# Feed-forwards on Trainium2: all up tiles before all down tiles, and each high weight streaming both parts as 512 columns

## The chip, the cores and the metric

One core of one Trainium2 chip runs the kernel. The metric is the device time of one execution in microseconds, as the median of runs. TensorE multiplies matrices (a weight load and a matmul are two instructions; results go to the banks of PSUM, `ps` in the kernel, eight banks of 128 x 512 fp32), VectorE and ScalarE work element by element, SyncE issues the DMAs of the weights.

## The reference

Two chains of layers over 256 tokens of width 1024, all in fp32: a block with a gated feed-forward, a hybrid attention mixer, cross attention and a second gated feed-forward, and then an RWKV layer, a squared-ReLU feed-forward, a sliding-window attention and a second squared-ReLU feed-forward. What matters here are the four feed-forwards:

```
x = x + 0.5 * swiglu(rmsnorm(x, ffn1_norm), w_gate, w_up, w_down)    # D_FF = 2816, again as ffn2
swiglu(h, w_gate, w_up, w_down) = (silu(h @ w_gate) * (h @ w_up)) @ w_down
x = x + square(relu(rms_norm(x, ln_mlp) @ w1)) @ w2                  # FFN_DIM = 4096, mlp1 and mlp2
```

## The kernel before

Activations are kept turned: 128 channels on the partitions, tokens along a row, `e.x` as 8 chunks of 128 x 256. Every weight comes as a tile of 1 MB (128 x 2048 fp32) in one fixed stream of 204 tiles. `feed` (L253) issues the DMAs from SyncE into a ring of four tiles; each waits until the tile four places earlier has been split (L263). To keep fp32 accuracy with the faster format `fp32r`, every number is split in two parts: ScalarE copies half a tile (1024 columns) into `tile_hi` (`heads_after`, L295, instruction L305) and VectorE subtracts that from the tile to give `tile_lo` (`rests_after`, L310, instruction L315). There are `SPLIT = 4` slots of half a tile, so a split waits until TensorE is done with the half tile four halves earlier. Activations (`hT`, the normed input, and `hidden`, the inner values) are split in the same way.

`product` (L353 to L357) is the core: three matmuls for one chunk of 128 weights rows and 128 weight columns, high by high, high weights by low activations, low weights by high activations, each with a weight load of its own and 256 columns, all three summed in the same half of a bank. The names in the profile give the activation first and the weight second (`ps<-hT_lo,tile_hi`). A tile has 16 products, 48 matmuls.

`ffn_stage` (L651) does a feed-forward in steps of 256 inner channels: 11 in ffn1 and ffn2 (a gate tile, an up tile, a down tile for each), 16 in mlp1 and mlp2 (an up tile and a down tile). The down tile of step j follows the up tiles of step j + 2 (`LAG = 2`), so up and down tiles take turns; the stream of weights has the same order. The up results of a step lie in one bank for each tile (banks 0 to 3), the down results add up in banks 4 to 7 over the whole stage. The inner values of three steps are kept (`hid`, `depth = 3`).

Gated: VectorE multiplies the gate's bank by the token's norm factor (L768), ScalarE takes Silu (L726), VectorE scales the up bank (L771) and multiplies the two (L774). Squared ReLU: ScalarE takes Relu out of the bank (L731), VectorE scales (L780) and squares (L781). Then ScalarE makes the high part (L736) and VectorE the low one (L789). All engines work in the order in which the program is written, so a split between two of these steps stands in the line with them.

At the end, the last down tile goes through the banks in pairs of output chunks, four blocks. For each block VectorE adds the bank to `e.x` (`add_to_residual`, L514 or L516), ScalarE makes the next section's high input and the squares (L548, L554), VectorE the low input (`rest_of_gained`, L524). The next section's first product waits for the first block's low input (`x_arrives`), its second tile's middle for the sum of squares (L597, L599, asked for by TensorE at L608).

Of the kernel before, what the change touches and what calls it, by code (L numbers as in the profile page):

```python
# [49 lines left out]
LAG = 2  # L50
# [8 lines left out]
AT_WEIGHTS, AT_MOVING, AT_INPUT, AT_FIRST_SLOT = 224, 160, 160, 128  # L59
# [84 lines left out]

class Unit:
# [18 lines left out]
def build(nc, a, out):  # L164
    ctx = ExitStack()
    with ctx:
# [19 lines left out]
        def over(name, tensor, shape, dtype=F32):  # L186
            return nc.alloc_sbuf_tensor_at(f"{name}{nc.next_id()}", shape, dtype, offset=places[tensor.name])

        def pair(stack, name, shape, place=AT_MOVING):
            return tuple(sb(stack, f"{name}_{part}{nc.next_id()}", shape, F32R, place) for part in ("hi", "lo"))  # L190
# [9 lines left out]
        e.hT = pair(ctx, "hT", [P, KC, SEQ], AT_INPUT)  # L200
        e.spare = tuple(over("spare", part, [P, KC, SEQ]) for part in e.hT)
# [4 lines left out]
        e.w_hi, e.w_lo = pair(ctx, "tile", [P, SPLIT, HALF], AT_WEIGHTS)  # L206
# [25 lines left out]
        ffn_stage(e, "mlp2", D_FF2, False, 1.0, None)  # L232
# [62 lines left out]
def heads_after(e, act, done):  # L295

    while may_split(e.hi_issued, done):
# [7 lines left out]
        act.activation(e.w_hi[:, n % SPLIT, :], e.ring[:, tile % RING, span(n % 2, HALF)],  # L305
# [4 lines left out]
def rests_after(e, dve, done):  # L310

    while may_split(e.lo_issued, done):
        n = e.lo_issued
        dve.wait_ge(e.tile_hi.handle, n + 1)
        dve.tensor_tensor(e.w_lo[:, n % SPLIT, :], e.ring[:, CUT[n // 2] % RING, span(n % 2, HALF)],  # L315
                          e.w_hi[:, n % SPLIT, :].bitcast(F32), ALU.subtract).then_inc(e.tile_lo.handle, 1)
        e.lo_issued += 1
# [12 lines left out]
def arrived(e, pe, g, half):  # L330

    n = 2 * place_in_cut(g) + half
    pe.wait_ge(e.tile_lo.handle, n + 1)
    return e.w_hi[:, n % SPLIT, :], e.w_lo[:, n % SPLIT, :]


def chunks_of(pair):
    return tuple(part.rearrange("p (k n) -> p k n", k=KC) for part in pair)
# [14 lines left out]
def product(pe, out, left, right, start, stop):  # L353

    pe.matmul(out, left[0], right[0], start=start, stop=False)  # L355
    pe.matmul(out, left[0], right[1], start=False, stop=False)  # L356
    return pe.matmul(out, left[1], right[0], start=False, stop=stop)  # L357
# [10 lines left out]
def cut(pair, *index):  # L368
    return tuple(part[index] for part in pair)
# [31 lines left out]
def col_to_natural(e, pe, g, src, bank):  # L401
# [3 lines left out]
    w = tuple(part[:, n:n + 2, :].rearrange("p m (k n) -> p m k n", k=KC) for part in (e.w_hi, e.w_lo))  # L405
# [100 lines left out]
def add_to_residual(e, dve, b, scale, last_tile, bank=4):  # L506
# [3 lines left out]
    else:  # L510
        multiplied(e, dve, last_tile)
    xs = e.x[:, two(b), :].rearrange("p m n -> p (m n)")
# [16 lines left out]
def tail_vector(e, dve, scale, outs, last_tile, bank=4):  # L529


    for n in range(6 if outs else 4):
        if n < 4:
            add_to_residual(e, dve, n, scale, last_tile, bank)
# [116 lines left out]
def ffn_stage(e, section, width, gated, scale, outs):  # L651
# [5 lines left out]
    per = 3 if gated else 2  # L657
    g0 = FIRST[section]
    depth = 3
    act_done, whole_ready, hi_ready, hidden_ready, scaled, chain = (  # L660
        e.sig(x) for x in ("gate_ready", "hidden_whole_ready", "hidden_hi_ready", "hidden_ready", "gate_scaled", "dve_step"))
    hT = e.hT

    def up_tile(j, which):
        return g0 + (per - 1) * j + max(j - LAG, 0) + which

    def down_tile(j):
        return g0 + (per - 1) * min(j + LAG + 1, steps) + j

    def up_bank(j, which):  # L670

        return 2 * (j % 2) + which if gated else (0, 2, 1, 3)[j % 4]

    end = down_tile(steps - 1)
    all_squared = e.sig("squared").since(4)

    with Open(nc) as block, ExitStack() as stack:
        hid = [e.pair(stack, f"hidden{n}", [P, 2, SEQ], AT_MOVING if n else AT_FIRST_SLOT) for n in range(depth)]
        whole = e.sb(stack, f"hidden_whole{nc.next_id()}", [P, 2, 2 * SEQ])
        tmp = e.sb(stack, f"gate{nc.next_id()}", [P, 2, 2 * SEQ])  # L680

        def slot(part, j):
            return hid[j % depth][part][:, :, :].rearrange("p m n -> p (m n)")

        @block.sync
        def _(sp):
            feed(e, sp, g0 + per * steps)

        @block.tensor
        def _(pe):  # L690
            def down(j):
                pe.wait_ge(*hidden_ready.at(j + 1))
                row_to_T(e, pe, down_tile(j), hid[j % depth], 0, j == 0, j == steps - 1)

            for j in range(steps):
                if gated and j >= 2:

                    pe.wait_ge(*hidden_ready.at(j - 1))
                if not gated and j >= 4:

                    pe.wait_ge(*act_done.at(j - 3))
                for which in range(per - 1):
                    nth = (per - 1) * j + which
                    if nth == 0:
                        first_to_T(e, pe, up_tile(j, which), hT, up_bank(j, which))
                    elif nth == 1:
                        col_to_T(e, pe, up_tile(j, which), hT, up_bank(j, which), between=lambda: scale_sums(e, pe, 7))
                        scale_spread(e, pe, 7)
                    else:
                        col_to_T(e, pe, up_tile(j, which), hT, up_bank(j, which))  # L710
# [2914 lines left out]
```

## Time and profile before

| | us |
|---|---|
| median of 3 runs | 1413.38 (1409.81 to 1413.94) |
| span of the profiled execution | 1422.4 |
| what lies around the span of that execution | not given by the page |
| TensorE busy | 1372.8 (97%), 12692 matmuls |
| TensorE's weight loads busy | 1314.1 (92%) |
| VectorE busy | 913.7 (64%) |
| ScalarE busy | 706.0 (50%) |
| read from HBM | 219.55 MB, 155 GB/s over the span |

The profile is of one execution, whose span is 9.0 us longer than the median of the runs. Busy time is the union of an engine's instructions; matmuls overlap in it, so how often one starts (count over the length of a window) says more than how long one lasts. A row of the timeline gives start, length, engine, line, operation, output and inputs, count of merged instructions, and in brackets the idle time before it and what ended that. In the stretches used here the granted TensorE clock is 1.00 of 2.4 GHz.

### The profile page before, as it was taken

The page shows a single profiled execution, that of the slowest core. Times are in us where ns is not written, and L with a number is a line of the kernel's source. Part 1 is how long each engine was busy: PE and PEld are TensorE (multiplying, and loading weights), DVE is VectorE, ACT ScalarE, POOL GpSimd, SP SyncE. Part 2 cuts the span into 40 slices and gives each one's busy share as a digit, 9 for nine tenths or more (in the row PEclk, how much of TensorE's full clock was granted, in tenths as well). Part 3 has the DMA queues.
Part 4 walks back from the last instruction along what each step waited for, and adds up shares of the span by engine and source line. Part 5 has one row for each costly group of instructions (what it writes and reads, how often), then busy time and mean ns, then how long its engine had stood idle before and what let it go on. Part 6 is the DMA issues. An engine that isn't in the chain of part 4 may idle for free. (4 is left out here: it accounts for less than half of the span.)

```text
span 1422.4 us, 28871 instructions
## 1 busy us (share of the span) xinstructions
PE 1372.8 (97%) x12692; PEld 1314.1 (92%) x12692; DVE 913.7 (64%) x1419; ACT 706.0 (50%) x1098; POOL 8.2 (1%) x14
## 2 busy tenths in 40 slices
PE   7999999999899999999999899999999996999999
PEld 7999999888799999999998677889999995999999
DVE  4665566557785546666588763667666668666664
ACT  5444455356564446444458333446444466554442
POOL 0000000000000000000000010000000000000000
PEclk9999999999999999999999998999999999999999
DMA  7555555461344344655524021114555541255552
GB/s 272 208 179 191 194 180 179 182 264 60 119 178 178 129 151 156 214 182 197 199 85 176 31 91 60 61 60 167 190 197 207 190 149 60 94 204 178 178 184 84
DMA packets 33109, 222.48 MB, mean 156 GB/s; under 512 B 3879, under 2 KB 5295, under 8 KB 6616
## 3 DMA queue, kind: packets, MB, share of 16 engines
q1 hardware_dynamic: 31928, 219.57, 42.7%
q8 instruction: 100, 1.64, 0.4%
q10 hardware_dynamic: 1056, 1.07, 0.2%
q14 instruction: 25, 0.20, 0.0%
HBM read 219.55 MB, written 1.07 MB: 155 GB/s over the span
## 5 line engine op out<-in xcount | busy, mean ns | idle before, releaser
L315 DVE TENSOR_TENSOR tile_lo<-ring,tile_hi 128x1024 fp32r<-128x1024 f32 x388 | 466.0, 1222 | 276.8 <-ACT tile_hi L305 276.2
L305 ACT ACTIVATE tile_hi<-ring 128x1024 fp32r<-128x1024 f32 x388 | 399.5, 1053 | 250.8 <-PE ps L357 245.8
L355 PE MATMUL ps<-hT_hi,tile_hi 128*128 128x256 f32 x1664 | 467.5, 281 | 5.0 <-DVE tile_lo L315 1.8
L356 PE MATMUL ps<-hT_lo,tile_hi 128*128 128x256 f32 x1664 | 463.4, 278 | 0.0
L357 PE MATMUL ps<-hT_hi,tile_lo 128*128 128x256 f32 x1664 | 463.4, 278 | 0.0
L355 PEld LDWEIGHTS ps<-hT_hi,tile_hi 128*128 128x128 f32 x1664 | 315.0, 189 | 10.6 <-issue 4.6
L356 PEld LDWEIGHTS ps<-hT_lo,tile_hi 128*128 128x128 f32 x1664 | 312.9, 188 | 0.0
L357 PEld LDWEIGHTS ps<-hT_hi,tile_lo 128*128 128x128 f32 x1664 | 312.7, 188 | 0.0
L355 PE MATMUL ps<-hidden_hi,tile_hi 128*128 128x256 f32 x864 | 241.2, 279 | 0.0
L357 PE MATMUL ps<-hidden_hi,tile_lo 128*128 128x256 f32 x864 | 241.2, 279 | 0.0
L356 PE MATMUL ps<-hidden_lo,tile_hi 128*128 128x256 f32 x864 | 241.2, 279 | 0.0
L355 PEld LDWEIGHTS ps<-hidden_hi,tile_hi 128*128 128x128 f32 x864 | 163.5, 189 | 0.0
L356 PEld LDWEIGHTS ps<-hidden_lo,tile_hi 128*128 128x128 f32 x864 | 162.4, 188 | 0.0
L357 PEld LDWEIGHTS ps<-hidden_hi,tile_lo 128*128 128x128 f32 x864 | 162.3, 188 | 0.0
L736 ACT ACTIVATE hidden_hi<-hidden_whole 128x512 fp32r<-128x512 f32 x54 | 34.2, 633 | 114.1 <-DVE hidden_whole L774 65.8
L789 DVE TENSOR_TENSOR hidden_lo<-hidden_whole,hidden_hi 128x512 fp32r<-128x512 f32 x54 | 37.4, 692 | 39.3 <-ACT hidden_hi L736 26.2
L780 DVE TENSOR_TENSOR hidden_whole<-gate,token_scale 128x512 f32<-128x512 f32 x32 | 22.1, 692 | 32.4 <-ACT gate L731 32.4
L731 ACT ACTIVATE gate<-ps 128x512 f32<-128x512 f32 x32 | 19.0, 595 | 42.8 <-PE ps L357 42.8
L1064 ACT ACTIVATE scores<-scores,lane_stats 128x128 f32<-128x128 f32 (+3 forms) x80 | 35.4, 445 | 8.8 <-DVE lane_stats L1090 8.8
L355 PE MATMUL ps<-y_turned,tile_hi 128*128 128x256 f32 x128 | 35.8, 280 | 2.9 <-DVE tile_lo L315 2.9
L726 ACT ACTIVATE gate<-gate 128x512 f32<-128x512 f32 x22 | 13.9, 632 | 46.1 <-DVE gate L768 46.1
L356 PE MATMUL ps<-y_turned,tile_hi 128*128 128x256 f32 x128 | 35.4, 277 | 0.0
(467 smaller groups left out, 1997.5 us busy)
## 6 DMA issues: line engine op xcount, KB each, us to landing
ring<-stream SPq DMA_DIRECT2D x204, 1024.0 KB, 4.8
x_sb<-x SPq DMA_DIRECT2D x4, 256.0 KB, 4.0
bias<-f_dram ACTq DMA_DIRECT2D x1, 1024.0 KB, 8.1
fox_bias<-forget_dram SPq DMA_DIRECT2D x1, 1024.0 KB, 6.2
squares<-mem SPq DMA_DIRECT2D x1, 1024.0 KB, 4.7
out<-x_sb SPq DMA_DIRECT2D x4, 256.0 KB, 2.2
const_sb<-const SPq DMA_DIRECT2D x1, 581.0 KB, 9.8
small_sb<-small SPq DMA_DIRECT2D x1, 493.5 KB, 9.5
```

Source lines behind the costliest of these rows:

```text
L305: act.activation(e.w_hi[:, n % SPLIT, :], e.ring[:, tile % RING, span(n % 2, HALF)], ACT.Copy).then_inc(e.tile_hi.handle, 1)
L315: dve.tensor_tensor(e.w_lo[:, n % SPLIT, :], e.ring[:, CUT[n // 2] % RING, span(n % 2, HALF)], e.w_hi[:, n % SPLIT, :].bitcast(F32), ALU.s ...
L355: pe.matmul(out, left[0], right[0], start=start, stop=False)
L356: pe.matmul(out, left[0], right[1], start=False, stop=False)
L357: return pe.matmul(out, left[1], right[0], start=False, stop=stop)
L726: act.activation(tmp[:, j % 2, :], tmp[:, j % 2, :], ACT.Silu).then_inc(*act_done.one())
L731: act.activation(tmp[:, j % 2, :], e.ps[:, up_bank(j, 0), :], ACT.Relu).then_inc(*act_done.one())
L736: act.activation(slot(0, j), whole[:, j % 2, :], ACT.Copy).then_inc(*hi_ready.one())
L780: link.done(dve.tensor_tensor(halves_of(both), halves_of(tmp[:, j % 2, :]), scale_pairs(e), ALU.mult))
L789: dve.tensor_tensor(slot(1, j), both, slot(0, j).bitcast(F32), ALU.subtract).then_inc(*hidden_ready.one())
L1064: x = act.activation(summed(step)[:, lane], summed(step)[:, lane], ACT.Exp, bias=st[:, 0, lane:lane + 1], accum_out=st[:, 1, lane:lane + 1])
```

## The change

The four feed-forwards run all up tiles first and then all down tiles, and the weight stream is laid out so. The inner values of every step are kept (`hidden`, 11 or 16 steps, high and low part side by side). High and low parts of all activations now lie one behind the other in one tensor (`Pair`), so one matmul can read both. `wide_product` loads the high weights once and streams 512 columns, the high and the low activations, into the two halves of a bank; a second matmul loads the low weights and streams the 256 high columns into the first half. A result thus takes a whole bank, and its two halves have to be added: for an up tile ScalarE copies the second half out and VectorE adds the first, before the scaling; at the end of the stage `add_to_residual` adds both halves to `x`, one after the other. Up tiles go round through all eight banks in four pairs, and the down results take all eight. Squared ReLU is now a maximum and scaling on VectorE and a Square on ScalarE. All other sections keep `product`; in the sliding-window stage three banks are renumbered.

```diff
+def wide_product(pe, bank, left, right, start, stop):
+    def low(stop):
+        return pe.matmul(bank[:, 0:SEQ], left.lo, right.hi, start=False, stop=stop)
+    if stop:
+        low(False)
+    mm = pe.matmul(halves_of(bank), left.hi, right.both, start=start, stop=stop)
+    return mm if stop else low(False)
...
+    if wide:                                   # add_to_residual
+        xs = e.x[:, two(b), :]
+        for half in range(2):
+            x = dve.scalar_tensor_tensor(out=xs, in0=e.ps[:, pair_of(b), span(half, SEQ)], scalar=scale, in1=xs,
+                                         op0=ALU.mult, op1=ALU.add)
+            if half == 0:
+                Chain(dve, e.sig("dve_step")).done(x)
+        x.then_inc(*e.sig("residual_added").one())
+        return
...
+def pair_of(n, first=0):
+    at = 2 * ((n + first) % 4)
+    return slice(at, at + 2)
...
         def _(pe):                             # ffn_stage, TensorE
+            first_up()
+            up(1, between=lambda: scale_sums(e, pe, scale_bank))
+            scale_spread(e, pe, scale_bank)
+            for n in range(2, count):
+                if n == 3:
+                    pe.wait_ge(*e.sig("scale_ready").at(1))
+                if n >= 4:
+                    pe.wait_ge(*summed.at(n - 3))
+                up(n)
...
+            halves = [arrived(e, pe, down0, k) for k in range(2)]
+            pe.wait_ge(*hidden_ready.at(1))
+            up_last = [max(n for n in range(count) if bank_of(m) in range(8)[up_banks(n)]) for m in range(KC)]
+            for m in sorted(range(KC), key=lambda m: up_last[m]):
+                pe.wait_ge(*summed.at(up_last[m] + 1))
+                for k in range(2):
+                    mm = down(halves[k], k, 0, m, start=k == 0)
+            mm.then_inc(*e.tile_done.one(2))
+            for j in range(1, steps - 1):
                 pe.wait_ge(*hidden_ready.at(j + 1))
...
+            def copy_low(n):                   # ScalarE
+                tile_after(e, act, g0 + n)
+                if n >= 2:
+                    act.wait_ge(*(consumed if gated else whole_ready).at(n - 1))
+                act.activation(part[:, n % 2, :, :], e.ps[:, up_banks(n), SEQ:2 * SEQ], ACT.Copy).then_inc(*low_copied.one())
+                heads_after(e, act, 2 * (g0 + n) + 2)
...
+                    copy_low(2 * j)
+                    act.wait_ge(*consumed.at(2 * j + 1))
+                    act.activation(gate[:, j % 2], gate[:, j % 2], ACT.Silu).then_inc(*act_done.one())
+                copy_low(ups * j + ups - 1)
                 act.wait_ge(*whole_ready.at(j + 1))
+                if not gated:
+                    act.activation(whole[:, j % 2], whole[:, j % 2], ACT.Square).then_inc(*act_done.one())
+                    act.wait_ge(*act_done.at(j + 1))
+                act.activation(hidden[:, j, 0], whole[:, j % 2], ACT.Copy).then_inc(*hi_ready.one())
...
+            def add_low(n):                    # VectorE
+                rests_before(e, dve, g0 + n + 1)
+                dve.wait_ge(*low_copied.at(n + 1))
+                dve.tensor_tensor(part[:, n % 2], e.ps[:, up_banks(n), 0:SEQ], part[:, n % 2], ALU.add).then_inc(*summed.one())
+                dve.wait_ge(*summed.at(n + 1))
...
+                    add_low(2 * j)
+                    dve.tensor_tensor(gate[:, j % 2], part[:, 0], scale_pairs(e), ALU.mult).then_inc(*consumed.one())
+                    rests_after(e, dve, 2 * (g0 + 2 * j) + 2)
+                    add_low(2 * j + 1)
+                    dve.tensor_tensor(whole[:, j % 2], part[:, 1], scale_pairs(e), ALU.mult).then_inc(*consumed.one())
...
+                    add_low(j)
+                    dve.scalar_tensor_tensor(out=whole[:, j % 2], in0=part[:, j % 2], scalar=0.0, in1=scale_pairs(e),
+                                             op0=ALU.max, op1=ALU.mult).then_inc(*whole_ready.one())
+                rests_after(e, dve, 2 * (g0 + ups * (j + 1)))
                 dve.wait_ge(*hi_ready.at(j + 1))
+                dve.tensor_tensor(hidden[:, j, 1], whole[:, j % 2], hidden[:, j, 0].bitcast(F32),
                                   ALU.subtract).then_inc(*hidden_ready.one())
```

## Rows read from the trace of the kernel before

**Rows 1.** The page, part 1: busy us of each engine, share of the span, instructions.
```profile
PE 1372.8 (97%) x12692; PEld 1314.1 (92%) x12692; DVE 913.7 (64%) x1419; ACT 706.0 (50%) x1098; POOL 8.2 (1%) x14
```

**Rows 2.** Windows inside ffn1, ffn2, mlp1, mlp2: length, busy us (instructions) by engine.
```profile
core 0: us, PE busy (x) PEld busy (x) DVE busy (x) ACT busy (x) POOL busy (x), PEclk, DMA share, GB/s
60.00:180.00 120.00, 120.00 (x1020) 120.00 (x1019) 71.41 (x71) 51.03 (x56) 0.00 (x0) 1.00 0.53 189
560.00:700.00 140.00, 140.00 (x1232) 140.00 (x1232) 88.32 (x90) 63.59 (x71) 0.00 (x0) 1.00 0.56 196
1000.00:1120.00 120.00, 120.00 (x1054) 120.00 (x1054) 75.30 (x78) 57.79 (x66) 0.00 (x0) 1.00 0.53 193
1270.00:1400.00 130.00, 130.00 (x1105) 130.00 (x1105) 79.46 (x81) 60.35 (x70) 0.00 (x0) 1.00 0.50 179
```

**Rows 3.** Timeline, TensorE or its loads, three places, plain fp32: start, length, count.
```profile
258.92 3.59 PE L1281 MATMUL ps<-bias,flip_sb 128*128 128x512 f32 x8
...
800.10 4.94 PEld L2258 LDWEIGHTS ps<-ring,mixed_values 128*128 128x128 f32 x23
...
498.21 1.03 PE L1791 MATMUL ps<-const_sb,bias 128*128 128x128 f32 x8
```

**Rows 4.** Groups by line and shape, plain fp32 matmuls: busy us, mean ns.
```profile
L1281 PE MATMUL ps<-bias,flip_sb 128*128 128x512 f32 x8 | 3.6, 592 | 0.0
...
L1791 PE MATMUL ps<-const_sb,bias 128*128 128x128 f32 x16 | 2.1, 272 | 0.0
```

**Rows 5.** Timeline of TensorE and its loads in an up tile of ffn1.
```profile
60.03 0.28 PE L355 MATMUL ps<-hT_hi,tile_hi 128*128 128x256 f32 x1
60.04 0.19 PEld L356 LDWEIGHTS ps<-hT_lo,tile_hi 128*128 128x128 f32 x1
```

**Rows 6.** Timeline of TensorE's loads, mixer stage, loads of 32 columns.
```profile
227.71 0.11 PEld L356 LDWEIGHTS ps<-hT_lo,misc_hi 128*32 128x32 f32 x1
227.82 0.11 PEld L357 LDWEIGHTS ps<-hT_hi,misc_lo 128*32 128x32 f32 x1
```

**Rows 7.** Groups by line and shape: count | busy us, mean ns | idle before them.
```profile
L315 DVE TENSOR_TENSOR tile_lo<-ring,tile_hi 128x1024 fp32r<-128x1024 f32 x388 | 466.0, 1222 | 276.8 <-ACT tile_hi L305 276.2
L789 DVE TENSOR_TENSOR hidden_lo<-hidden_whole,hidden_hi 128x512 fp32r<-128x512 f32 x54 | 37.4, 692 | 39.3 <-ACT hidden_hi L736 26.2 <-PE ps L357 13.1
...
L514 DVE TENSOR_TENSOR x_sb<-ps,x_sb 128x512 f32<-128x512 f32 x24 | 16.1, 687 | 10.2 <-PE ps L357 10.2
...
L305 ACT ACTIVATE tile_hi<-ring 128x1024 fp32r<-128x1024 f32 x388 | 399.5, 1053 | 250.8 <-PE ps L357 245.8 <-DMA ring<-stream 3.3 <-PEq L2432 1.5
L736 ACT ACTIVATE hidden_hi<-hidden_whole 128x512 fp32r<-128x512 f32 x54 | 34.2, 633 | 114.1 <-DVE hidden_whole L774 65.8 <-DVE hidden_whole L781 48.2
...
L731 ACT ACTIVATE gate<-ps 128x512 f32<-128x512 f32 x32 | 19.0, 595 | 42.8 <-PE ps L357 42.8
L554 ACT ACTIVATE squares<-x_sb 128x512 f32<-128x512 f32 x32 | 19.0, 617 | 1.7 <-DVE x_sb L516 1.7
```

**Rows 8.** Timeline around the end of ffn1: VectorE, then TensorE.
```profile
199.68 1.28 DVE L516 SCALAR_TENSOR_TENSOR x_sb<-ps,x_sb 128x512 f32<-128x512 f32 x2
201.69 0.69 DVE L516 SCALAR_TENSOR_TENSOR x_sb<-ps,x_sb 128x512 f32<-128x512 f32 x1 [0.72 <-PE ps L357]
...
203.71 2.46 DVE L524 SCALAR_TENSOR_TENSOR hT_lo<-x_sb,small_sb,hT_hi 128x256 fp32r<-128x256 f32 x6
...
203.31 0.36 PE L355 MATMUL ps<-hT_hi,tile_hi 128*128 128x256 f32 x1 [0.25 <-DVE hT_lo L524]
```

**Rows 9.** Timeline of the sum of squares after ffn1: VectorE, then TensorE.
```profile
209.77 0.69 DVE L599 TENSOR_TENSOR squares<-squares 128x512 f32<-128x512 f32 x1
...
211.57 0.95 PE L608 MATMUL ps<-ones,squares 128*128 128x1 f32 x8
```

**Rows 10.** Timeline at the end of mlp2: VectorE, then TensorE.
```profile
1419.43 0.69 DVE L514 TENSOR_TENSOR x_sb<-ps,x_sb 128x512 f32<-128x512 f32 x1 [0.73 <-PE ps L357]
...
1419.12 0.28 PE L357 MATMUL ps<-hidden_hi,tile_lo 128*128 128x256 f32 x1
```

More of the change, by code:

```diff
@@ L49 @@
 LEAST = -3e38
-LAG = 2
 RING = 4
@@ L368, in cut @@
 def cut(pair, *index):
-    return tuple(part[index] for part in pair)
+    both = None if pair.both is None else pair.both[(index[0], slice(None), *index[1:])]
+    return Pair(pair.hi[index], pair.lo[index], both)
 ALL = slice(None)
@@ L648, in halves_of, with bank_of, ffn_stage @@
     return bank.rearrange("p (m n) -> p m n", m=2)
-def ffn_stage(e, section, width, gated, scale, outs):
+def pair_of(n, first=0):
+    at = 2 * ((n + first) % 4)
+    return slice(at, at + 2)
+def bank_of(m, first=0):
+    return pair_of(m // 2, first).start + m % 2
+def ffn_stage(e, section, width, gated, scale, outs, first=0):
     e.stage()
@@ L656, in ffn_stage @@
     steps = width // 256
[L657 removed]
+    ups = 2 if gated else 1
     g0 = FIRST[section]
[L659 to L668 removed]
@@ L685, in _ @@
         @block.sync
         def _(sp):
-            feed(e, sp, g0 + per * steps)
+            feed(e, sp, end + 1)
         @block.tensor
         def _(pe):
-            def down(j):
-                pe.wait_ge(*hidden_ready.at(j + 1))
[L693 to L710, printed above, removed]
-                if j >= LAG:
-                    down(j - LAG)
@@ L713, in _, with up @@
-            mark_tail(e)
-            for j in range(steps - LAG, steps):
-                down(j)
+            def up(n, between=None):
+                for m in range(2):
+                    w = chunks_of(arrived(e, pe, g0 + n, m))
+                    for k in range(KC):
+                        mm = wide_product(pe, e.ps[:, bank_of(2 * (n % 4) + m, first), :], cut(w, ALL, k, ALL),
+                                          cut(hT, ALL, k, ALL), k == 0, k == KC - 1)
+                    mm.then_inc(*e.tile_done.one())
+                    if between and m == 0:
+                        between()
@@ L717, in _ @@
+            mark_tail(e)
+            pe.wait_ge(*hidden_ready.at(steps))
+            halves = [arrived(e, pe, end, k) for k in range(2)]
+            for m in range(KC):
+                for k in range(2):
+                    mm = down(halves[k], k, steps - 1, m, stop=k == 1)
+                if m % 2 == 1 and m < KC - 1:
+                    mm.then_inc(*e.sig("acc_ready").one())
+            mm.then_inc(*e.tile_done.one(2))
         @block.scalar
```

167 lines of the change are left out of this document (78 added, 89 removed).

## The prediction

> **What bounds the kernel now.** I read the page's busy shares first: TensorE 97%, its weight loads 92%, VectorE 64%, ScalarE 50% [rows 1]. TensorE bounds the kernel, and the question is what one of its instructions costs. So I cut out four stretches that lie wholly inside the four feed-forwards and counted matmuls [rows 2]. The reader is to see two prices there for the same instruction. In ffn1 and mlp2 a matmul of 256 columns starts every 120/1020 us = 117.6 ns and 130/1105 us = 117.6 ns; in ffn2 and mlp1 every 140/1232 us = 113.6 ns and 120/1054 us = 113.9 ns. The granted clock is 1.00 (2.4 GHz) in all four, and TensorE never idles in them, so I have no reason for the difference and carry both. 256 columns at 2.4 GHz are 106.7 ns. A matmul therefore costs 10.9 or 7 ns more than its columns, and a product (three matmuls) 352.9, 340.9, 341.6 and 352.9 ns in ffn1, ffn2, mlp1 and mlp2.
>
> **What the change does to a product.** It keeps the 768 columns and turns three pairs of load and matmul into two: high weights with 512 columns, low weights with 256. There are 33 tiles in each gated feed-forward and 32 in each other, 16 products each: 528, 528, 512, 512, together 2080 products. Each loses one load and one matmul start. What that is worth hangs on what the 7 to 11 ns are. The trace has no matmul of 512 columns with this number format, so I bound it.
>
> The nearest rows are plain fp32 matmuls, which take two clocks a column. Eight of 512 columns take 3.59 us [rows 3]; less the length of the last one, 0.59 [rows 4], that is 3.00/7 = 429 ns from start to start. 23 loads under 256-column matmuls take 4.94 us, (4.94 − 0.19)/22 = 216 ns apart; 8 matmuls of 128 columns (1.03 − 0.27)/7 = 109 ns [rows 3, 4]. Their columns alone are 426.7, 213.3 and 106.7 ns, so 2.3 to 2.7 ns are added whatever the length. The middle one is the important one: its stream is exactly as long as that of a 512-column matmul of this kernel (213.3 ns), a 128x128 load runs under it, and it costs 216 ns. A load lasts 0.19 us from its start a few ns after the matmul before began [rows 5], so under 213 ns of stream it is over in time and under 107 ns it is not. That makes the 7 to 11 ns a load that comes a little late. After the change the load of the low weights hides under the 512 columns; only the load of the next high weights stays under 256. Then a product is 216 + 113.6 = 329.6 ns in the quick stretches and 216 + 117.6 = 333.6 ns in the slow ones.
>
> Against this speaks that matmuls with only 32 weight columns, whose loads last 0.11 us, also start 0.11 us apart [rows 6]: the added time doesn't shrink with the load. If it is a fixed price of each matmul of this format, a product saves just one of it, 6.9 to 10.9 ns. I keep this as a rival. The bounds of the price are: nothing saved (the excess goes with columns), and 216 + 109 = 325 ns (both matmuls lose it). I take 329.6 and 333.6, since the one row whose stream has the right length says 216.
>
> Saved on products: ffn1 528 × (352.9 − 333.6) = 10.2 us; ffn2 528 × (340.9 − 329.6) = 6.0; mlp1 512 × (341.6 − 329.6) = 6.1; mlp2 512 × 19.3 = 9.9. Sum 32.2 us.
>
> The Trainium skill (TensorE: Matmul & The Clock Gate, "Back-to-back issue gap") has a rule that speaks against such a gain: a warm matmul costs its columns over 2.4 GHz plus about 2.5 ns. By it three times 256 columns are 327.5 ns and 512 with 256 are 325, only 2.5 ns saved a product, 5 us in all. The trace agrees with the rule in plain fp32 [rows 3] and not in the feed-forwards, at 340.9 to 352.9 ns; by the rule, what stands above it there is something that the change need not touch.
>
> **VectorE and ScalarE while up tiles run.** Before, a third or half of the tiles are down tiles, which ask only for splits. Now all up tiles come in a row, and the low sums add work. VectorE's operations on 512 elements cost 0.69 us, whether from the banks or not; a split half 1.22; ScalarE's split half 1.05, its copy from the banks 0.60, its others 0.62 to 0.63 [rows 7].
> Squared ReLU, one up tile: VectorE 2 × 1.22 + 3 × 0.69 (sum, max-and-scale, low half) = 4.5 us; ScalarE 2 × 1.05 + 0.60 + 0.62 + 0.63 = 4.0 us; TensorE 16 × 0.330 = 5.3 us. Gated, two up tiles: VectorE 4 × 1.22 + 6 × 0.69 = 9.0, ScalarE 6.7, TensorE 10.6. Both fit, at 85% of VectorE. The closed round is longer than the work, as both engines wait for each other in order. For squared ReLU it is: sum 0.69, scale 0.69, ScalarE's square 0.63 and high half 0.63, next split's high half 1.05, VectorE's low half 1.22: 4.9 us (handovers between the engines not counted), 0.4 less than TensorE's 5.3. For a gated step the round adds up to 3 × 0.69 (second sum, scaling, product), 0.63, 1.05, 1.22, 2 × 0.69 (first sum, scaling), 0.63, 1.05, 1.22: 9.3 against 10.6. TensorE doesn't wait for a tile's sum until four tiles later (eight banks in four pairs), and a split is due 1.5 tiles after its slot is free. So I cost this at nothing, with TensorE's stream as its cover; if the round were longer than a tile, each of the 76 up tiles (22 + 22 + 16 + 16) would cost the excess.
>
> **From up to down.** The first down tile takes the pairs of banks in the order in which they are freed; the last pair is asked for after three others, 12 products = 4.0 us after the last up tile, and its copy and sum take 0.60 + 0.69 and up to one split half in between, 1.05: under 2.6 us. The last inner value is due ten or more tiles later. Nothing. The down tiles leave VectorE 2.4 us in 5.3. The stream of weights is 1 MB a tile; 5.3 us a tile asks 198 GB/s, and such stretches ran at 179 to 196 with the DMA engines busy 50 to 56% of the time [rows 2]. The queue waits for the split of four tiles before, as it did, now with nothing else between. Nothing.
>
> **The end of each feed-forward.** Here the change costs. A pair of banks now needs two additions to x, the second waiting for the first: one more of 0.69 us in each of four blocks. At ffn1's end VectorE goes from its first addition at 199.68 to the last low half at 206.17 with 0.72 us idle; the next section's first product comes at 203.31 after a wait for the first low half [rows 8]. That one stands behind three additions, now six: 3 × 0.69 − 0.72 = 1.4 us later. Everything after on VectorE is 4 × 0.69 − 0.72 = 2.1 us later, and the sum of squares, which TensorE asks for at 211.57 [rows 9], is ready at 210.46 before and 212.6 after, when TensorE asks at 213.0: no second stall. mlp1's end has the same form. So 1.5 us each, 3.0. ffn2 has no such overlap: its sums of squares stand behind the last addition, 1.0 us (0.69, and some backlog, as two additions, 1.38, no longer fit in 4 × 0.333 = 1.33 us of TensorE). At mlp2's end the output leaves after the last addition, which before began at 1419.43 behind the last matmul at 1419.12 [rows 10]: 0.9 us. Sum 4.9 us.
>
> **Sum.** 1422.4 − 32.2 + 4.9 = 1395.1 us, 27.3 less. The profiled span is 9.0 us longer than the median of the runs, 1413.4, and the page gives no other time for it; I take the difference over: 1386 us.
>
> **Rivals.**
> 1. Each matmul has a fixed price beyond its columns. The 32-column loads speak for it, the 216 ns against. Saved: 528 × 10.9 + 528 × 6.9 + 512 × 7.2 + 512 × 10.9 = 18.7 us, less 4.9: 1400 us.
> 2. The excess goes with the columns (say, how fast they are read), or is something that the change doesn't touch. Nothing is saved, 4.9 lost: 1418 us. For it: the excess is the same for 32 and 128 weight columns. Against: plain fp32 adds 2.3 to 2.7 ns at every length [rows 3], not a share of it. The mild form: a product saves only that price of one matmul, 2.5 ns × 2080 = 5.2 us, and the time stays at 1413 us. This is also where the rule of the Trainium skill cited above (TensorE: Matmul & The Clock Gate) would end.
> 3. VectorE and ScalarE bound the up tiles: slower, where the mechanism is the closed round, its place the 76 up tiles. It decides from an excess of 27.3/76 = 0.36 us a tile, a round of 5.7 us for squared ReLU; for an excess of 0.6 us a tile it costs 46 and ends at 1432. Against: idle time stands before most splits now (276 us of VectorE behind ScalarE's high half), for: that idle time is partly this round.
> 4. All stretches become quick ones and both matmuls lose their excess, 325 ns a product: 528 × 27.9 + 528 × 15.9 + 512 × 16.6 + 512 × 27.9 = 45.9 us, less 4.9: 1372 us.
>
> **How the numbers follow.** The forecast has 0.50, the fixed price 0.20, rival 4 0.08, the columns 0.10 (half of it the mild form), the engines 0.12. A difference of 0.3% (4.2 us) is about what a measurement can tell from no change. Faster: forecast, fixed price and rival 4, 0.78, and 0.02 of the engines, with an excess well under 0.36 us: 0.80. Same: the mild form 0.05 and 0.02 of the engines: 0.07. Slower: the columns' 0.05 and the engines' 0.08: 0.13. The range goes from 1374, near rival 4, to 1411, short of the columns' case, and leaves out about 0.2.
>
> **What would show it.** 512-column matmuls 216 ns apart from the next, the 256-column ones 113 to 118; at 224 and 114 to 118 the fixed price is right, at 227 to 235 the columns. TensorE without idle time in the stretches of up tiles, VectorE there at 80 to 88%; a wait of TensorE for the low half of a split in them shows rival 3. The next section's first product 1.4 us later behind the last matmul of ffn1 and mlp1. Wrong would be the forecast also if the slow price of ffn1 and mlp2 moved to the others, 4 ns in each of two matmuls of 1040 products: up to 8 us.

## The result and the profile after

The changed kernel takes 1441.64 us (median of 4 runs, 1438.63 to 1447.47), the kernel before beside it 1413.66 (4 runs, 1409.81 to 1416.64): ratio 1.020, 95% interval 1.0167 to 1.0233. It is 28 us slower; the forecast was 27 us faster. The profiled execution of the changed kernel took 1447.47 us, 1.3 more than its span of 1446.2; by span it is 23.8 us longer than the one before.

The page, part 1 [rows 1]:

```profile
PE 1390.4 (96%) x10612; PEld 1235.9 (85%) x10612; DVE 950.2 (66%) x1479; ACT 751.3 (52%) x1174; POOL 8.2 (1%) x14
```

2080 matmuls and as many loads are gone (12692 to 10612), and TensorE is busy for longer. Windows inside the feed-forwards, two for each (up tiles, then down tiles) in the order ffn1, ffn2, mlp1, mlp2, with the columns of [rows 2]:

```profile
60.00:130.00 70.00, 70.00 (x399) 60.95 (x398) 53.42 (x61) 38.86 (x50) 0.00 (x0) 1.00 0.56 187
150.00:190.00 40.00, 40.00 (x229) 34.77 (x228) 17.36 (x15) 15.28 (x15) 0.00 (x0) 1.00 0.56 188
560.00:650.00 90.00, 90.00 (x513) 78.39 (x512) 72.64 (x85) 52.59 (x68) 0.00 (x0) 1.00 0.58 199
680.00:720.00 40.00, 40.00 (x229) 34.73 (x228) 17.58 (x15) 14.85 (x14) 0.00 (x0) 1.00 0.56 188
1000.00:1060.00 60.00, 60.00 (x342) 52.27 (x341) 49.46 (x57) 41.30 (x57) 0.00 (x0) 1.00 0.59 201
1080.00:1150.00 70.00, 70.00 (x398) 60.77 (x398) 30.62 (x25) 25.92 (x26) 0.00 (x0) 1.00 0.56 191
1290.00:1340.00 50.00, 50.00 (x286) 43.50 (x285) 41.37 (x48) 35.03 (x47) 0.00 (x0) 1.00 0.58 192
1370.00:1430.00 60.00, 60.00 (x341) 52.14 (x340) 26.31 (x22) 22.28 (x21) 0.00 (x0) 1.00 0.42 141
```

A product is now two matmuls, so by these counts it costs between 2 × 40/229 = 349 ns and 2 × 60/341 = 352 ns. A window also counts the matmuls that reach in over its edge, which makes short windows read 1 to 4 ns low; from the first start to the last one the trace gives 352.4 to 352.5 ns a product in the up tiles and 353.3 in the down tiles of all four. Before it was 352.9, 340.9, 341.6 and 352.9 ns [rows 2], by counts as well. TensorE has no idle time in any of them, and VectorE is busy 76 to 83% in the up tiles. The timeline of TensorE in an up tile of ffn1 shows which of the two matmuls is dear:

```profile
60.01 0.28 PE L382 MATMUL ps<-hT_pair,tile_pair 128*128 128x256 f32 x1
60.13 0.40 PE L386 MATMUL ps<-hT_pair,tile_pair 128*128 128x512 f32 x1
60.36 0.28 PE L382 MATMUL ps<-hT_pair,tile_pair 128*128 128x256 f32 x1
60.48 0.40 PE L386 MATMUL ps<-hT_pair,tile_pair 128*128 128x512 f32 x1
```

From a 512-column start to the next matmul 0.23 to 0.24 us, from a 256-column one 0.12. The prediction's text names this case: 512 columns at 227 to 235 ns mean that "the columns" is right.

The end of ffn1, VectorE and then TensorE, answers to [rows 8, 9]:

```profile
199.81 4.05 DVE L547 SCALAR_TENSOR_TENSOR x_sb<-ps,x_sb 128x512 f32<-128x512 f32 x6
203.78 0.87 DVE L565 SCALAR_TENSOR_TENSOR hT_pair<-x_sb,small_sb,hT_pair 128x256 fp32r<-128x256 f32 x2
204.57 1.41 DVE L547 SCALAR_TENSOR_TENSOR x_sb<-ps,x_sb 128x512 f32<-128x512 f32 x2
...
202.72 0.39 PE L386 MATMUL ps<-hidden,tile_pair 128*128 128x512 f32 x1
204.81 0.35 PE L372 MATMUL ps<-hT_pair,tile_pair 128*128 128x256 f32 x1 [1.70 <-DVE hT_pair L565]
...
206.83 0.39 PE L372 MATMUL ps<-hT_pair,tile_pair 128*128 128x256 f32 x1 [0.37 <-DVE hT_pair L565]
```

Six additions in a row stand ahead of the first low half, as predicted, and TensorE's wait grows from 0.25 to 1.70 us. A second wait comes at 206.83, behind the last two additions. At the end of mlp1 the first wait is the same, and there the clock falls after it (timeline of TensorE, then a window of the changed kernel and one of the kernel before at the same place in the program):

```profile
1154.88 0.39 PE L386 MATMUL ps<-hidden,tile_pair 128*128 128x512 f32 x1
1156.97 0.36 PE L372 MATMUL ps<-kvT_pair,tile_pair 128*128 128x256 f32 x1 [1.70 <-DVE kvT_pair L565]
...
1157.00:1171.00 14.00, 14.00 (x73) 14.00 (x74) 10.88 (x20) 8.06 (x16) 0.00 (x0) 0.56 0.38 142
```

```profile
1141.00:1149.00 8.00, 8.00 (x70) 8.00 (x71) 7.94 (x17) 8.00 (x16) 0.00 (x0) 1.00 0.40 133
```

73 matmuls took 14 us at a granted clock of 0.56, mostly the lower level of 1.2 GHz; before, 70 took 8 us at 1.00. The difference is 14 − 73 × 8/70 = 5.7 us.

Where the 23.8 us of span came from, read off the same landmarks (starts of the same instructions) in both timelines: 2.4 by the sum of squares after ffn1 (asked for at 214.00, before at 211.57), 1.8 more by the start of ffn2 (a half-clock spell near 428 us is longer), 4.6 in ffn2, 5.6 in mlp1, 1.6 at its end, 6.1 in the section of shared keys and values behind it, 1.7 in mlp2 and the end of the kernel. The last ffn1 matmul begins at the same time as before, 202.72 against 202.78: where the old price was already the slow one, the wide product changed next to nothing.

### The profile page after: what moved, and what is told of

Same layout as the page of the kernel before. It is cut to its first block and busy times, and to the rows that moved or that the text cites. A ratio compares the mean times of both kernels' runs of the same rounds, so it can differ in the third digit from the quotient of the medians.

```text
span 1446.2 us, 24871 instructions
## 1 busy us (share of the span) xinstructions
PE 1390.4 (96%) x10612; PEld 1235.9 (85%) x10612; DVE 950.2 (66%) x1479; ACT 751.3 (52%) x1174; POOL 8.2 (1%) x14
## 5 line engine op out<-in xcount | busy, mean ns | idle before, releaser
L331 DVE TENSOR_TENSOR tile_pair<-ring,tile_pair 128x1024 fp32r<-128x1024 f32 x388 | 470.4, 1222 | 294.3 <-ACT tile_pair L321 293.6
L321 ACT ACTIVATE tile_pair<-ring 128x1024 fp32r<-128x1024 f32 x388 | 405.2, 1055 | 282.2 <-PE ps L382 164.1
L386 PE MATMUL ps<-hT_pair,tile_pair 128*128 128x512 f32 x1216 | 421.6, 397 | 1.7 <-DVE tile_pair L331 0.8
L382 PE MATMUL ps<-hT_pair,tile_pair 128*128 128x256 f32 x1216 | 317.6, 281 | 0.0
L386 PE MATMUL ps<-hidden,tile_pair 128*128 128x512 f32 x864 | 303.3, 397 | 0.0
L386 PEld LDWEIGHTS ps<-hT_pair,tile_pair 128*128 128x128 f32 x1216 | 219.3, 188 | 45.4 <-issue 2.7
L382 PEld LDWEIGHTS ps<-hT_pair,tile_pair 128*128 128x128 f32 x1216 | 228.3, 188 | 12.7
L382 PE MATMUL ps<-hidden,tile_pair 128*128 128x256 f32 x864 | 237.5, 281 | 0.0
L386 PEld LDWEIGHTS ps<-hidden,tile_pair 128*128 128x128 f32 x864 | 160.4, 188 | 37.2
L382 PEld LDWEIGHTS ps<-hidden,tile_pair 128*128 128x128 f32 x864 | 162.2, 188 | 2.8
L372 PE MATMUL ps<-hT_pair,tile_pair 128*128 128x256 f32 x448 | 128.3, 286 | 4.7 <-DVE hT_pair L565 2.1
L373 PE MATMUL ps<-hT_pair,tile_pair 128*128 128x256 f32 x448 | 125.3, 280 | 0.0
L374 PE MATMUL ps<-hT_pair,tile_pair 128*128 128x256 f32 x448 | 125.3, 280 | 0.0
L372 PEld LDWEIGHTS ps<-hT_pair,tile_pair 128*128 128x128 f32 x448 | 84.9, 189 | 9.6 <-issue 4.9
L843 DVE TENSOR_TENSOR up_part<-ps,up_part 128x512 f32<-128x512 f32 x76 | 52.5, 690 | 52.7 <-ACT up_part L805 52.6
L373 PEld LDWEIGHTS ps<-hT_pair,tile_pair 128*128 128x128 f32 x448 | 84.9, 189 | 0.0
L374 PEld LDWEIGHTS ps<-hT_pair,tile_pair 128*128 128x128 f32 x448 | 84.8, 189 | 0.0
L805 ACT ACTIVATE up_part<-ps 128x512 f32<-128x512 f32 x76 | 45.2, 595 | 70.5 <-PE ps L386 70.5
```

Source lines behind the costliest of these rows:

```text
L321: act.activation(e.w.hi[:, n % SPLIT, :], e.ring[:, tile % RING, span(n % 2, HALF)], ACT.Copy).then_inc(e.tile_hi.handle, 1)
L331: dve.tensor_tensor(e.w.lo[:, n % SPLIT, :], e.ring[:, CUT[n // 2] % RING, span(n % 2, HALF)], e.w.hi[:, n % SPLIT, :].bitcast(F32), ALU.s ...
L372: pe.matmul(out, left.hi, right.hi, start=start, stop=False)
L373: pe.matmul(out, left.hi, right.lo, start=False, stop=False)
L374: return pe.matmul(out, left.lo, right.hi, start=False, stop=stop)
L382: return pe.matmul(bank[:, 0:SEQ], left.lo, right.hi, start=False, stop=stop)
```

## The experiments

Two theories stood at the start. The forecast's: an added time of 7 to 11 ns for each load that is not hidden. Its rival: a price that goes with the columns. To them came a question that the trace raised: why ffn2 and mlp1 lost what they had.

**1. The price by itself.** A kernel that leaves the computation out and only runs short streams of matmuls of this number format, most of them 8 products long, with operands at many positions in SBUF (0 to 224 bytes past a multiple of 256) and nothing else going on. Its kinds, in short:

```diff
+if kind == "three":   # high*high, high*low, low*high, 256 columns each
+elif kind == "wide":  # high * (high and low), 512 columns; low * high, 256
+elif kind == "only512":
+elif kind == "cols":  # 256 columns, but 32 or 64 weight columns
```

> Leaves the whole computation out; it only streams fp32r matmuls with nothing else running: three matmuls of 256 columns per product, 512 with 256, 512 alone, 256 columns with 32 to 128 weight columns, 32 to 256 columns with 128 weight columns, at several positions of the operands in their rows. Theory C (the price goes with the columns): 512 alone starts every 226 to 236 ns, exactly twice 256 alone (113 to 118), with 128 or 32 weight columns alike. Theory of the forecast (a late load): 512 every 216 ns, 256 with 32 weight columns 109. A fixed price: 512 every 220 to 224. If the position of the operands chooses between the quick price (113.3) and the slow one (117.8), each price keeps to its positions; if it is a state that lasts, the same positions show both.

Measured from start to start: three of 256 columns 113.3 to 120.2 ns each, by position and by what ran before (the same operands gave 118 ns at first and 113.3 in eleven repeats after a pause); the wide product 346 to 356 ns, so at none of 24 pairs of positions at the 340 of the quick stages, but at eight of them at 346 to 347; 512 columns alone 229 to 235 at seven positions and 227 at the eighth. Here is the wide product at one of the eight pairs:

```profile
280.43 0.28 PE L52 MATMUL ps<-mvg,wtf 128*128 128x256 f32 x1
280.54 0.39 PE L51 MATMUL ps<-mvg,wtf 128*128 128x512 f32 x1
280.77 0.28 PE L52 MATMUL ps<-mvg,wtf 128*128 128x256 f32 x1
280.89 0.39 PE L51 MATMUL ps<-mvg,wtf 128*128 128x512 f32 x1
```

With 256 columns and only 32 weight columns it is 113.8 ns at one position and 120.0 at another, where 128 weight columns gave 114.0 and 116.8. So a load of a quarter of the size saves nothing and a 512-column stream costs about what two of 256 do. The late load is out, and both prices exist without any other engine at work.

**2. The wide product alone undone**, halves and sums kept:

```diff
-    mm = pe.matmul(halves_of(bank), left.hi, right.both, start=start, stop=stop)
+    pe.matmul(bank[:, 0:SEQ], left.hi, right.hi, start=start, stop=False)
+    mm = pe.matmul(bank[:, SEQ:2 * SEQ], left.hi, right.lo, start=False, stop=stop)
```

> The changed kernel with the wide product alone undone: three matmuls of 256 columns again, the low activations by the high weights still into the second half of the bank, all else as changed. Theory C: the same time as the changed kernel within 5 us, so 1436 to 1447, since the columns are the same; less by up to 12 us if ffn2 and mlp1 fall back to the quick price. Theory of the forecast: 2080 loads more that come late, 11 to 19 ns each, so 1465 to 1480.

1428.3 us (6 runs, 1416.77 to 1433.51), ratio 1.0056 (1.0006 to 1.0107): 13 us less than the changed kernel by medians, 20 by ratios, which is the fairer measure, since the two ran beside different runs of the kernel before. Windows of ffn1 and ffn2, then the one behind mlp1's end:

```profile
60.00:130.00 70.00, 70.00 (x597) 70.00 (x596) 53.52 (x62) 39.24 (x49) 0.00 (x0) 1.00 0.52 183
560.00:650.00 90.00, 90.00 (x797) 90.00 (x796) 74.03 (x85) 54.01 (x70) 0.00 (x0) 1.00 0.58 205
...
1142.00:1156.00 14.00, 14.00 (x73) 14.00 (x72) 10.41 (x19) 7.96 (x16) 0.00 (x0) 0.54 0.38 140
```

ffn1 runs at 117.3 ns, ffn2 at 112.9 (the two others as ffn2). More loads, more matmuls, and faster; the forecast's theory had asked for 1465 to 1480. VectorE and ScalarE have the same work as in the changed kernel, so they are not what slowed it. The last row: mlp1's end kept its wait (1.82 us idle here) and the low clock behind it.

**3. Up tiles wide, down tiles as three matmuls in one half**, with one addition at the end:

```diff
-                return wide_product(pe, e.ps[:, bank_of(m), :], ...)          # down
+                return product(pe, e.ps[:, bank_of(m), 0:SEQ], ...)
-        for half in range(2):
-            x = dve.scalar_tensor_tensor(out=xs, in0=e.ps[:, pair_of(b), span(half, SEQ)], ...)
+        x = dve.scalar_tensor_tensor(out=xs, in0=e.ps[:, pair_of(b), 0:SEQ], ...)
```

> The changed kernel with down tiles as three matmuls of 256 columns into one half of each bank, so that a block needs one addition to x again; up tiles stay wide. Theory C: down tiles cost the same, the ends of the feed-forwards get back 1.5 to 2.5 us each, and the idle time of 2 us before the shared keys and values, after which TensorE runs at half clock, shrinks to 0.5: 6 to 14 us less than the changed kernel, 1427 to 1435. If the half clock stays, 1435 to 1438. Theory of the forecast: 864 products lose 11 to 19 ns each, 9 to 16 us more, less the same 6 to 14: about the same time as the changed kernel.

1424.95 us (10 runs, 1422.36 to 1431.57), ratio 1.0049 (1.0022 to 1.0075), 2 us below the 1427 to 1435 of theory C. Windows of ffn1 and mlp1, up and down:

```profile
60.00:130.00 70.00, 70.00 (x399) 60.92 (x399) 53.41 (x63) 39.76 (x50) 0.00 (x0) 1.00 0.56 193
150.00:190.00 40.00, 40.00 (x355) 40.00 (x355) 17.64 (x16) 15.94 (x15) 0.00 (x0) 1.00 0.60 207
...
1000.00:1060.00 60.00, 60.00 (x342) 52.27 (x341) 49.45 (x57) 41.52 (x56) 0.00 (x0) 1.00 0.57 198
1080.00:1130.00 50.00, 50.00 (x443) 50.00 (x442) 22.57 (x19) 19.62 (x19) 0.00 (x0) 1.00 0.56 193
```

In one execution and one feed-forward, the wide half costs 2 × 70/399 = 351 ns a product and the other 3 × 40/355 = 338 (352.5 and 340.0 from start to start). This is the clearest pair of rows of the study: the price changes where the form of the product does. It also refutes one line of theory C, that down tiles cost the same either way: all four down halves ran at 340.0.

**4. The order alone**: all up tiles, then all down tiles, every product three matmuls into one half, no copies, no sums, one addition.

```diff
-                        mm = wide_product(pe, e.ps[:, bank_of(...), :], ...)
+                        mm = product(pe, e.ps[:, bank_of(...), 0:SEQ], ...)
-                act.activation(part[:, n % 2, :, :], e.ps[:, up_banks(n), SEQ:2 * SEQ], ACT.Copy)...
-                dve.tensor_tensor(part[:, n % 2], e.ps[:, up_banks(n), 0:SEQ], part[:, n % 2], ALU.add)...
```

> The order alone: all up tiles, then all down tiles, inner values kept, but every product three matmuls into one half of a bank, no copy and no sum of halves on ScalarE and VectorE, one addition to x. Theory C: as the kernel before within 5 us where the price of a column is as before; up to 13 us more if ffn2 and mlp1 keep the slow price, 1410 to 1427. If waits of VectorE and ScalarE in the up tiles were the cause of the loss, this is 20 us or more faster than the run with only the down tiles changed.

1413.0 us (10 runs, 1407.34 to 1421.75), ratio 0.9959 (0.9932 to 0.9986), up and down tiles of all four feed-forwards at 113.3 ns a matmul from start to start. The order costs nothing, so all of the loss is in the wide product and its halves.

**5. Long streams.** 144 matmuls after each short pause, four pairs of positions, computation left out again:

> Leaves the whole computation out; long runs of products after a pause, nothing else running, at four pairs of operand positions that were quick or slow for 256 columns: three matmuls of 256 into one half; the wide product of the changed kernel; the wide product with the low weights first; 512 alone; three matmuls of 256 into two halves. Theory P (the quick price of 0.443 ns a column is a rhythm between the stream of columns and something else, which equal matmuls can lock into and alternating lengths can't): three matmuls reach 113.3 ns at the positions 160/224 and both wide products never go below 353 ns a product (117.7 per 256 columns); 512 alone may reach 227. Theory A (it is only the position): at some pair the wide product reaches 340 too.

Three of 256 columns were at 113.3 ns in 13 of 16 streams and at 117.8 in 3, at positions that showed both; the wide product was at 353.3 ns (117.8 per 256 columns) in all 16, whichever of its matmuls came first; 512 columns alone at 233.3 in all 8. So equal streams have two rhythms and mostly take the quick one. The wide product has the slow price only, at these four pairs of positions as in the kernel; the pairs that gave 346 to 347 ns in experiment 1 were not run as long streams, nor in the kernel.

**6. The changed kernel without the second additions** (the second halves of the down results are left out of `x`; TensorE's work is the same):

> The changed kernel without the second additions to x at the ends of the feed-forwards: the second halves of the down results (high weights by low activations) are left out of x; everything else, the wide products too, stays. The end theory (the second additions cost 1.5 to 2.5 us at each end and the long idle time before the shared keys and values costs a spell of half clock, 6 us): 8 to 14 us less than the changed kernel, so 1427 to 1434. If the ends are not the cause: 1438 to 1442.

1432.78 us (4 runs, 1430.43 to 1438.63), ratio 1.0108 (1.0069 to 1.0148): 9 us less than the changed kernel by medians, 13 by ratios, as the theory of the ends had it. mlp1's end:

```profile
1153.76 0.39 PE L386 MATMUL ps<-hidden,tile_pair 128*128 128x512 f32 x1
1154.43 0.36 PE L372 MATMUL ps<-kvT_pair,tile_pair 128*128 128x256 f32 x1 [0.28 <-DVE kvT_pair L562]
...
1155.00:1164.00 9.00, 9.00 (x81) 9.00 (x80) 8.93 (x17) 8.57 (x17) 0.00 (x0) 1.00 0.39 125
```

With 0.28 us of idle time in place of 1.70 the clock stays at 1.00. The feed-forwards still ran at 351 ns a product.

**7. Is it where the operands lie?** The kernel before, its first slot of inner values 32 bytes further on:

```diff
-AT_WEIGHTS, AT_MOVING, AT_INPUT, AT_FIRST_SLOT = 224, 160, 160, 128
+AT_WEIGHTS, AT_MOVING, AT_INPUT, AT_FIRST_SLOT = 224, 160, 160, 160
```

> The kernel before with one number changed: the first of the three slots of inner values begins at the same position in its 256 bytes as the other two (160 instead of 128). If that slot is what throws ffn1 and mlp2 into the slow price, all four feed-forwards run at 113.3 ns and 1040 products cost 12 ns less: 12 us less than the kernel before, 1406 beside 1418. If the rhythm is lost in another way, no difference.

1420.4 us (10 runs) against 1417.08 of before on that chip, ratio 1.0006 (0.9967 to 1.0045). Slow were ffn1 and ffn2 this time, quick mlp1 and mlp2, where the profile of before has ffn1 and mlp2 slow. The 12 us are not there: which stage is quick is not set by that position.

**8. The order alone again**, beside the same runs of the kernel before:

> The order alone once more, beside the kernel before with its first slot moved, for the interval: 0.3 to 0.8% faster than the kernel before, since all four feed-forwards run at 113.3 ns a matmul where the kernel before has 117.8 in two of them.

1417.24 us (12 runs, 1402.66 to 1426.18), ratio 0.9988 (0.9958 to 1.0018). In this profile ffn2 was slow (80 us x682: 117.3 ns), the others quick. The gain of experiment 4 is not confirmed. One stage that flips is worth 528 × 12 ns = 6 us, so a good part of the scatter of these kernels may be such flips (their executions weren't profiled one by one).

**9. Which lengths are dear?** Long streams as in 5, of other lengths, the 512 columns now in one piece:

```diff
+for kind, count in (("three", 48), ("len256_256", 70), ("len512", 70), ("len512_256", 48), ("len384_384", 48), ("len256_192", 80)):
```

> The kernel's computation is left out: long streams of matmuls with nothing else running, two of each kind at three pairs of operand positions, each after a short pause. Six kinds: three matmuls of 256 columns a product; single matmuls of 256 columns; of 512 columns that lie in one piece (until now the 512 lay in two pieces, high and low part); 512 in one piece with 256 by turns; 384 alone; 256 and 192 by turns. Prices per 256 columns: 113.3 ns quick, 117.6 ns slow. Theory A, only streams of equal matmuls of at most 256 columns can become quick: 256 alone is quick in most runs, 512 in one piece stays at 235 ns (117.5 per 256), 512 with 256 at 353 ns a pair, 384 at 176 ns, 256 with 192 at about 206 ns a pair. Theory B, the two pieces of the 512 columns are what keeps the wide product slow: 512 in one piece is quick in most runs, 227 ns, and 512 with 256 takes 340 ns. If the two prices are a chance of each run whatever the lengths, every kind shows both.

Windows of 256 alone, 512 alone, 512 with 256, and 384 alone (columns: length, TensorE, loads, ScalarE, GpSimd, granted clock, DMA):

```profile
88.00:103.00 15.00, 15.00 (x135) 15.00 (x134) 0.00 (x0) 0.00 (x0) 1.00 0.00 1
122.00:136.00 14.00, 14.00 (x62) 11.28 (x61) 0.00 (x0) 0.00 (x0) 1.00 0.00 0
...
156.00:171.00 15.00, 15.00 (x87) 13.02 (x86) 0.00 (x0) 0.00 (x0) 1.00 0.01 1
...
192.00:206.00 14.00, 14.00 (x83) 14.00 (x82) 0.00 (x0) 0.00 (x0) 1.00 0.00 0
```

From start to start, six streams of each: 256 columns 113.3 ns, 384 173.3 or 174.6, 512 233.3, 512 with 256 by turns 353.3 a pair, 256 with 192 by turns 230.0. Lying in one piece does not help: theory B falls. Theory A is not confirmed in its numbers either: its 235 ns was 1.7 too high, its 176 for 384 columns 1.4 to 2.7 too high, and its 206 for 256 with 192 was 24 too low. And one thing was in neither: 512 with 256 costs 6.7 ns more than the two alone, 233.3 + 113.3 = 346.6.

**10. More lengths, and eight and eight**:

> The kernel's computation is left out: long streams of matmuls as before, of 128, 160, 192, 224, 320 and 448 columns alone, 384 with 128 by turns, and eight of 512 columns followed by eight of 256, again and again. The run before gave, from start to start, 113.3 ns for 256 alone, 173.3 to 174.6 for 384, 233.3 for 512, but 353.4 for 512 with 256 by turns, 6.7 more than 233.3 + 113.3, and 230 for 256 with 192. Theory A, the change of length between neighbours costs: eight and eight take 346.7 ns a product, 384 with 128 by turns costs over 7 ns more than the two alone, and each length alone has one steady price. Theory B, the price is the columns' own and 512 with 256 is only the slow rate of both: eight and eight take 353 ns a product.

128, 160, 192 and 224 columns cost 111.7 ns each, whatever the length; 320 cost 146.7, 448 cost 202.2. 384 with 128 by turns takes 285.0, just the two alone (173.3 + 111.7), where theory A had expected over 7 ns more: turns as such cost nothing there. Eight of 512 and then eight of 256 settle at 346.7 a product, as theory A says. Early in one of these streams:

```profile
219.34 2.03 PE L64 MATMUL ps<-mvf,wth 128*128 128x512 f32 x8
221.21 1.08 PE L66 MATMUL ps<-mvf,wth 128*128 128x256 f32 x8
222.13 2.02 PE L64 MATMUL ps<-mvf,wth 128*128 128x512 f32 x8
```

Eight of 512 last 221.21 − 219.34 = 1.87 us, eight of 256 last 0.92: 349 ns a product on this group, the second behind the pause; from the third on it is 346.7.

**11. The same in the kernel**: the changed kernel with highs and lows in rows of eight.

```diff
-                    for k in range(KC):
-                        mm = wide_product(pe, ..., k == 0, k == KC - 1)
+                    high_products(pe, bank, w, hT, [0], start=True)
+                    low_products(pe, bank, w, hT, range(KC))
+                    mm = high_products(pe, bank, w, hT, range(1, KC), stop=True)
```

> The changed kernel with the order of the matmuls changed in 118 of its 130 tiles (all but the first up tile, the first and the last down tile of each feed-forward): the wide matmuls of half a tile stand together and the 256-column ones with the low weights stand together, eight in a row (in an up tile one wide, eight low, seven wide). Same columns, loads and operations else. Theory A, the change of length between neighbours costs 6.7 ns a product: the stretches take 346.7 ns a product in place of 353.3, 1888 products x 6.7 ns = 12.6 us less: 1429 us. Theory B, the price goes with the columns alone: 1441.6 us, 353 ns a product.

Timeline in ffn1 and the window behind mlp1's end:

```profile
60.09 2.02 PE L392 MATMUL ps<-hT_pair,tile_pair 128*128 128x512 f32 x8
61.95 1.07 PE L399 MATMUL ps<-hT_pair,tile_pair 128*128 128x256 f32 x8
62.86 1.32 PE L392 MATMUL ps<-hT_pair,tile_pair 128*128 128x512 f32 x5
...
1149.00:1166.00 17.00, 17.00 (x83) 17.00 (x82) 11.65 (x19) 9.12 (x17) 0.00 (x0) 0.51 0.26 93
```

A product costs (62.86 − 60.09)/8 = 346 ns, as theory A says, and mlp1 ends at 1145.24, 9.6 us earlier than in the changed kernel; theory A gives 89 of the 118 tiles up to there, 89 × 16 × 6.7 ns = 9.5 us. The price is confirmed. The time came out at 1440.92 us (6 runs, 1429.4 to 1444.09), not 1429, but on a chip where the kernel before took 1421.77: ratio 1.0133 (1.0072 to 1.0194). That is 0.7%, 9.5 us, under the changed kernel's ratio, with intervals that overlap, so the gain in time is likely and not shown. A small part of it went to the clock: 83 matmuls took 17 us at 0.51, which is 17 − 83 × 8/70 = 7.5 us lost, 1.8 more than in the changed kernel.

## Why the prediction was wrong

**The step that failed** is the one that reads, "That makes the 7 to 11 ns a load that comes a little late." It rested on plain fp32 matmuls of 256 columns, whose stream is as long in time as 512 columns of this format, and which cost 216 ns [rows 3]. The analogy did not carry: 512 columns of this format cost 233.3 ns alone (experiments 5, 9; 227 to 235 by position in experiment 1) and mostly 235 beside 256-column ones, in the kernel as in an empty one. The price a column is nearly the same at every length from 256 on: 113.3/256 = 0.443, 146.7/320 = 0.458, 173.3/384 = 0.451, 202.2/448 = 0.451, 233.3/512 = 0.456 ns, against 0.417 at 2.4 GHz. Rival 2, with a chance of 0.10, had the mechanism; the row for it stood in the text, the 32-column loads with the same spacing [rows 6], and was outweighed by a row of another format.

**Product**: forecast 329.6 and 333.6 ns, measured 352.5 (up tiles) and 353.3 (down tiles). The 32.2 us of saving were nothing. The rule weighed in the prediction, of the Trainium skill (TensorE: Matmul & The Clock Gate, "Back-to-back issue gap"), columns over 2.4 GHz plus 2.5 ns, gives an estimate of 215.8 ns for 512 columns; the runs here disagree with it in this format, 233.3. The conclusion that the prediction drew from it, that fusing two matmuls saves next to nothing, held.

**What no rival had in full**: rival 2 ends at 1418 us, the result is 24 above. The text's last paragraph named half of it, the slow price moving to the other stages, "up to 8 us". It is more: ffn2 528 × (353 − 340.9) = 6.4 us, mlp1 512 × (353 − 341.6) = 5.8, together 12.2, since the slow price counts per 256 columns and so three times a product. (By landmarks 4.6 and 5.6.) The forecast's error was to carry the two prices as a fact of the stages. They are a fact of streams of equal 256-column matmuls, and the wide product, with its operands where the kernel has them, has only the slow one (experiments 2, 3, 5).

**The ends**: forecast 4.9 us, the sum of four small terms. The first product behind ffn1 and mlp1 came 1.5 to 1.6 us later, as worked out. Mis-sized were the rest: after ffn1 the last additions hold TensorE a second time, and the sum of squares is 2.4 us later, not 1.4; and the wait at mlp1's end is followed by 5.7 us lost to the clock. Experiment 6 puts all ends together at 9 to 13 us. That the clock hangs on that wait is well supported, not proved: three kernels with 1.70 to 1.82 us idle there (the changed one, experiments 2 and 11) had the low clock behind it, six with 0.26 to 0.30 (before, experiments 3, 4, 6, 7 and 8) did not. The same three kernels idled 1.61 to 1.71 us at ffn1's end and kept the full clock behind it, so idle time alone is not the whole condition.

**The sum, redone**: 12.2 on products, 9 at the ends by experiment 6 (its profiled span is 8.9 us shorter), 21 of the 23.8 us of span; the rest is the longer half-clock spell near 428 us and small change in mlp2. By medians the gap is 28, and the kernel before by itself runs between 1409 and 1417 there and up to 1431 elsewhere, so a few of the 28 may be its luck with the quick rhythm; no run shows that.

**What was right**: VectorE and ScalarE do not bound the up tiles (rival 3): TensorE is 100% busy there, with VectorE at 76 to 83%, where the forecast said 80 to 88; the two waits of 0.4 us for a low half, early in mlp1 and mlp2, are all there is. Going from up to down costs nothing. Rivals 1 and 4 are out with the forecast, for the same reason: they ask for 224 and 216 ns where 512 columns took 227 to 235.

**What stays open**: what makes a stream of equal matmuls quick or slow. It isn't the position of the inner values (experiment 7), nor other engines (1, 5), and it changes between repeats. Whether the wide product would run in the kernel at the 346 to 347 ns that eight pairs of positions gave in experiment 1: 6 ns on 2080 products would be 12 us (an estimate), and no run tried it. And whether the order alone is worth 0.4% or nothing: the two measurements gave 0.9959 and 0.9988.

## What to carry to other kernels

Price an instruction by a row of its own number format, or by a kernel of a few lines that measures it, before merging instructions; a row of another format with the same duration is no substitute. When one instruction shows two prices in one profile, ask which of them the new form can have, and count the loss of the cheap one as a term. Measure with the operands where the kernel will have them, in a stream as long as the kernel's. Additions in front of a handover cost more than their own time where the wait may also bring the clock down.

## What the runs showed of the hardware

- Long streams of 256-column fp32r matmuls ran at one of two prices at full clock, 113.3 or 117.8 ns, and where the feed-forwards have three matmuls a product, each kept the one it had from its first tiles to its end (experiments 2, 3, 4, 7, 8). Short streams showed others, up to 120.2 (experiment 1).
- From 128 to 224 columns a load and matmul of this format cost 111.7 ns, whatever the length (experiment 10).
- 512 with 256 columns by turns costs 6.7 ns a pair more than in rows of eight (353.3 and 346.7), in long streams at four pairs of positions and in the kernel; in short streams at eight other pairs it did not (346 to 347). 256 with 192 costs 5.0 more than alone (230.0 against 113.3 + 111.7); 384 with 128 costs nothing more.
- A quarter of the weight columns in a load does not shorten the spacing (113.8 and 120.0 ns with 32, 114.0 and 116.8 with 128).
